# A two-layer MLA/NSA transformer kernel on one core: a PSUM place for each of four attention units, and transposes three units behind the scores

## The reference

```
for l in range(2):
    proj = rms_norm(x, attn_norm[l]) @ w_in[l]
    q_lat, kv_lat, k_rope, nsa_q, nsa_kv, gate_logits = split(proj)
    o_mla = mla_attention(...)      # 8 heads, causal softmax(q k) v, q and k built from q_lat, kv_lat, k_rope
    o_nsa = nsa_attention(...)      # 8 heads: compressed keys (31 blocks), selected blocks, window; gated sum
    x = x + concat([o_mla, o_nsa]) @ w_out[l]
    x = x + conv_ffn(rms_norm(x, ffn_norm[l]), ...)
return rms_norm(x, final_norm)
```

## Time and profile before

| | |
|---|---|
| time, median of 3 runs | 1435.41 us (1433.96 to 1436.16) |
| time of the profiled execution | 1435.41 us |
| its span in the trace | 1433.7 us |
| PE busy | 1333.7 us, 93% |
| DVE busy, ACT busy, POOL busy | 755.4, 650.3, 69.7 us |
| mean granted TensorE clock | 0.977 |

### The profile page before, as it was taken

How to read it: one execution, slowest core, us unless ns; L and a number is a source line. 1 busy time by engine, 2 the same in 40 slices (tenths; PEclk the granted TensorE clock), 3 DMA queues, 4 the chain that set the end, 5 groups by cost and what they waited for, 6 DMA issues and landing times.

```text
span 1433.7 us, 20017 instructions
## 1 busy us (share of the span) xinstructions
PE 1333.7 (93%) x6756; PEld 1079.0 (75%) x6756; DVE 755.4 (53%) x1200; ACT 650.3 (45%) x1173; POOL 69.7 (5%) x153
## 2 busy tenths in 40 slices
PE   5997888999999999999999988798999999999996
PEld 5995665567888888888889865566788888887884
DVE  6445566745455555533363646766364555564333
ACT  4345455744444544422352545666354454453222
POOL 1013001000000000000000401100000000000000
PEclk9998988999999999999999999989999999999998
DMA  6320100021433333323133101000323333323211
GB/s 202 114 81 2 59 1 1 16 89 54 120 89 114 90 88 108 112 89 101 52 100 95 51 18 43 1 16 1 118 76 113 90 88 105 100 88 117 88 59 59
DMA packets 121492, 107.69 MB, mean 75 GB/s; under 512 B 3874, under 2 KB 110980, under 8 KB 121424
## 3 DMA queue, kind: packets, MB, share of 16 engines
q1 hardware_dynamic: 119200, 102.71, 23.6%
q0 software_dynamic: 1360, 3.45, 0.9%
q10 hardware_dynamic: 864, 0.66, 0.1%
HBM read 104.71 MB, written 2.10 MB: 74 GB/s over the span
## 4 chain that ended last, share of the span: by engine, by line
PE 82%; DVE 7%; issue 5%; ACT 4%; DMA 1%; SPq 0%; DVEq 0%; ACTq 0%
PE ps L1306 23%; PE ps L1308 23%; PE ps L1307 23%; PE ps L1466 3%; PE ps L1507 3%; ACT probs L785 2%; PE ps L1490 1%; PE ps L1450 1%; PE ps L1542 1%; DVE probs L1115 1%; DMA raw<-in_w_in_dram 1%; PE ps L1451 1%; DVE x L986 1%; ACT probs_t L795 1%; DVE nmax L1097 1%
## 5 line engine op out<-in xcount | busy, mean ns | idle before, releaser
L1306 PE MATMUL ps<-ht_hi,w_hi 128*128 128x512 f32 (+2 forms) x776 | 299.9, 386 | 20.4 <-DVE k_operand L1139 5.3
L1308 PE MATMUL ps<-ht_hi,w_lo 128*128 128x512 f32 (+2 forms) x776 | 298.4, 385 | 0.0
L1307 PE MATMUL ps<-ht_lo,w_hi 128*128 128x512 f32 (+2 forms) x776 | 298.3, 384 | 0.0
L533 DVE TENSOR_TENSOR w_lo<-raw,w_hi 128x1024 fp32r<-128x1024 f32 (+4 forms) x196 | 218.1, 1141 | 105.0 <-ACT w_hi L526 97.2
L526 ACT ACTIVATE w_hi<-raw 128x1024 fp32r<-128x1024 f32 (+4 forms) x196 | 186.5, 982 | 109.2 <-PE ps L1308 103.8
L1251 DVE SCALAR_TENSOR_TENSOR conv<-ps,cols,conv 128x510 f32<-128x510 f32 (+1 forms) x176 | 127.7, 746 | 180.0 <-ACT conv L890 173.9
L1306 PEld LDWEIGHTS ps<-ht_hi,w_hi 128*128 128x128 f32 x776 | 146.7, 189 | 49.2 <-issue 17.5
L1308 PEld LDWEIGHTS ps<-ht_hi,w_lo 128*128 128x128 f32 x776 | 147.2, 190 | 28.1
L1307 PEld LDWEIGHTS ps<-ht_lo,w_hi 128*128 128x128 f32 x776 | 147.0, 189 | 27.5
L1306 PE MATMUL ps<-w_hi,ht_hi 128*128 128x430 f32 (+1 forms) x392 | 147.8, 377 | 5.9 <-DVE ht_lo L973 5.3
L1307 PE MATMUL ps<-w_lo,ht_hi 128*128 128x430 f32 (+1 forms) x392 | 145.4, 371 | 0.0
(11 more groups left out here) (182 smaller groups left out, 1705.1 us busy)
## 6 DMA issues: line engine op xcount, KB each, us to landing
raw<-in_ffn_w_up_dram SPq DMA_DIRECT2D x88, 512.0 KB, 4.3
raw<-in_ffn_w_down_dram SPq DMA_DIRECT2D x44, 512.0 KB, 3.6
raw<-in_w_in_dram SPq DMA_DIRECT2D x32, 430.0 KB, 3.4
raw<-in_w_out_dram SPq DMA_DIRECT2D x16, 512.0 KB, 4.7
raw<-in_nsa_cmp_w_dram SPq DMA_DIRECT2D x8, 512.0 KB, 4.2
x<-in_x_dram SPq DMA_DIRECT2D x4, 512.0 KB, 6.3
out_dram<-probs SPq DMA_DIRECT2D x4, 512.0 KB, 2.6
raw<-in_mla_w_uq_dram SPq DMA_DIRECT2D x4, 384.0 KB, 3.2
```

Source lines behind the costliest of these rows:

```text
L533: last = nc.vector.tensor_tensor(d(w_lo)[:, :, d0:d1], r(raw)[:, :, r0:r1], d(w_hi)[:, :, d0:d1].bitcast(F32), ALU.subtract)
L1306: mm(o, lhs[0], rhs[0], start=start, stop=False)
L1307: mm(o, lhs[0], rhs[1], start=False, stop=False)
L1308: return mm(o, lhs[1], rhs[0], start=False, stop=stop)
```

## The change

There are three edits that belong together, and several that follow from them.

1. Every unit gets a PSUM place by its query block: block 3 banks 0 and 1, block 2 banks 2 and 3, block 1 bank 4, block 0 bank 5. The transposes are written over the unit's own scores. So `scores(u)` now waits for `evac_pt(u - 4)`, and `turn(u)` waits for its probabilities alone.
2. `turn` moves from two to three steps behind the scores, `values` from four to five.
3. In each step the order is turned round. PE issues `queries` or `keys`, `turn(s - 3)`, `values(s - 5)`, the side job, and `scores(s)` last. ACT issues `evac_pt(s - 3)`, then the side splits, and `exps(s)` last. DVE takes the bank 7 work of the same step first, then `row_max(s)`, `q_lo`, `scale_probs(s - 1)`.

The rest: units with both heads in one bank write each head's causal mask by a product of its own (NSA's did it with one for both); `BACK_STEP`, `CS_MAX_STEP`, `CS_SCALE_STEP` and `PC_STEP` come two steps later; the four value products of MLA and their evacuations are taken in the order 3, 1, 0, 2.

```diff
-LAG = 4
+LAG = 5
+T_LAG = 3
-CS_STEP, BACK_STEP, CS_MAX_STEP, CS_SCALE_STEP, PC_STEP = [15, 18], [19, 20], 21, 23, [25, 26]
+CS_STEP, BACK_STEP, CS_MAX_STEP, CS_SCALE_STEP, PC_STEP = [15, 18], [21, 22], 23, 25, [27, 28]
+V_ORDER = (3, 1, 0, 2)
...
-            n = (unit(u)[0] + 1) * P
-            if u >= U_MLA and 2 * n <= S:
-                return ps[:, 2 * (u % 2), 0:2 * n].rearrange("p (a n) -> p a n", a=2)
-            return ps[:, 2 * (u % 2):2 * (u % 2) + 2, 0:n]
+            i = unit(u)[0]
+            n = (i + 1) * P
+            if i < 2:
+                return ps[:, 5 - i, 0:2 * n].rearrange("p (a n) -> p a n", a=2)
+            return ps[:, 6 - 2 * i:8 - 2 * i, 0:n]
...
-                    if u >= 2:
-                        pe.wait_ge(exp_done, at(exp_done, l, u - 1))
+                    if u >= T:
+                        pe.wait_ge(pt_done, at(pt_done, l, u - T + 1))
...
-                    if u >= 1:
-                        pe.wait_ge(pt_done, at(pt_done, l, u))
+                    sc = score_banks(u)
                     for s in range(2):
                         for b in range(i + 1):
-                            last = nc.tensor.transpose(ps[:, 4 + s, b * P:(b + 1) * P],
+                            last = nc.tensor.transpose(sc[:, s, b * P:(b + 1) * P],
```

More of the change, by code:

```diff
@@ L821, in _ @@
                 for s in range(U + LAG):
[L822 to L833, removed]
+                    if 0 <= s - T_LAG < U:
+                        evac_pt(s - T_LAG)
                     if LAG <= s < U_MLA + LAG and (s - LAG) % T == T - 1:
@@ L838, in _ @@
                         evac_out(H // 2 + pair, 6 + pair % 2)
-                    if not early and 0 <= s - 2 < U:
-                        evac_pt(s - 2)
+                    if s < QK_STEPS and s % T == 1:
+                        k_hi(s // T + 1, 7)
+                    if s < QK_STEPS and s % 2 == 0:
+                        q_hi(s // 2 + 2)
                     if s in ITEM_STEP:
@@ L865, in _ @@
                         activate(pct[:, g, :], ps[:, 7, :], ACT.Copy).then_inc(pct_ready, 1)
+                    if s < U:
+                        exps(s)
+                    if s == 2:
+                        act.wait_ge(gate_in, at(gate_in, l, 1))
+                        activate(gates[:, :, :], gate_e[:, :, :], ACT.Exp, scale=-1.0).then_inc(gate_exp, 1)
+                    if s == CS_MAX_STEP + 1:
+                        act.wait_ge(cs_sub, at(cs_sub, l, 1))
+                        activate(scp, scp, ACT.Exp).then_inc(cs_exp, 1)
                     if s == U_MLA + 4 * T:
@@ L1168, in _ @@
                 for s in range(U + LAG):
-                    if s < U:
-                        row_max(s)
-                    if s - 1 in ITEM_STEP:
-                        item_lo(ITEM_STEP.index(s - 1))
-                    if s == HIDT_STEP + 1:
+                    if s < QK_STEPS and s % 2 == 0:
+                        q_rows(s // 2 + 2, 7)
+                    if s < QK_STEPS and s % T == 1:
+                        k_lo(s // T + 1, 7)
+                    if s in ITEM_STEP:
+                        item_lo(ITEM_STEP.index(s))
+                    if s == HIDT_STEP:
                         dve.wait_ge(hid_tp, at(hid_tp, l, 1))
@@ L1602, in _ @@
                             queries(2 * pair + (s % T) // 2, 7)
-                    if s >= LAG and s not in VALUES_FIRST and s % 2 == 1:
+                    if 0 <= s - T_LAG < U:
+                        turn(s - T_LAG)
+                    if s >= LAG and (s - LAG) % 2 == 1:
                         values(s - LAG)
-                    if 0 <= s - 2 < U:
-                        turn(s - 2)
-                    if T <= s <= QK_STEPS:
+                    if T - 1 <= s <= QK_STEPS:
                         if s < QK_STEPS and s % T == 1:
```

101 lines of the change are left out of this document (43 added, 58 removed).

## The result

The changed kernel is slower. It took 1446.78 us (median of 4 runs, 1445.29 to 1447.34), the kernel before 1435.36 us beside it (4 runs, 1433.96 to 1436.16): ratio 1.0093, 95% interval 1.0077 to 1.0110, so 11.4 us more. I had forecast 1432.0: a small gain, and it is a loss. The range, 1413 to 1447 us, takes in the time at its very edge, and only because I had stretched it for the slower rival.

The account below looks back on a forecast made before the run. PE was taken as the bound (busy 1333.7 of 1433.7 us), so only its idle time, half-clock time and work count. Second part -4.4, first +2.7: -1.7 us a layer, -3.4 for both, from 1435.4 to 1432.0 us; range 1413 to 1447.

Parts of the forecast that it names:

- the slower rival: Whole kernel: bank 7 ring with ACT and DVE takes more than the quiet part gives back; 1447 us, chance 0.3.
- Second part: -4.4 us: Quiet NSA units and stage end, per layer: 3.7 us less idle, 1.2 from drains, 0.5 added by extra causal products.
- only one transpose still comes some 0.3 us early: Quiet part: `turn` of the 512-column unit waits for `scale_probs`; 0.3 us in 4.75 rounds, second part's idle 2.2 us.
- the drains that were to give 1.2 us: Second part: each wait uncovers a pipeline drain of 0.17 us; about seven fewer waits give 1.2 us.
- The extra masks' 0.5: Second part: about ten extra causal products at some 0.05 us each add 0.5 us.
- signs of being wrong: Among them, quiet part: DVE's `scale_probs` over 0.5 us late for every unit would make DVE's order the bound.
- the low clock I put at 11.5 instead of 12.5: First part: loss from PE's half clock falls from 12.5 to 11.5 us, as waits are fewer but longer.
- My bound of 6 us either way: First part: low-clock loss may lie between half and one and a half of 12.5 us.
- The first part's waits: Steps 0 to 28: PE's waits sum to 29.8 us, less 0.3 for the earlier start, against 24.8 before.
- the ring: Steps 12 to 18: `item_lo`, maxima, exponentials, copy, `item_hi` in turn, about 5.6 us; waits 7.6 us, before 6.4.
- Gain everywhere: Whole kernel: long waits too come from scarce places; first part idle 18 us, 1400 to 1420 us, chance 0.2.
- The rule of the Trainium skill: Quiet part: by the rule it gains clock as well as bubbles; the prediction's sum took bubbles alone, clock already 1.00.

Follow-up runs that it names:

- the run that prices them: The kernel before, with a causal product for each head in the small NSA units instead of one for both: 1434.24 us, ratio 1.0003.
- softmax run: The changed kernel, with return, maxima and scaling of the compressed scores one step earlier: 1435.24 us, ratio 1.0025 to the kernel before.
- order and distances alone: The changed kernel with the old PSUM banks (two score buffers, common transpose banks): 1459.29 us, ratio 1.0193 to the kernel before.
- the places alone: The kernel before with the new PSUM places and own causal masks, old step order and distances: 1425.12 us, ratio 0.9943.
- each mend: Four edits to the changed kernel: `k_hi` first, late items behind maxima, scaling ahead of 384-column maxima, softmax a step earlier; all four together 1424.20 us, ratio 0.9945.
- selective scaling: The changed kernel; from step 29 DVE scales the 256-column unit ahead of the 384-column unit's row maxima: 1437.03 us, ratio 1.0024 to the kernel before.
- key first: The changed kernel, with `k_hi` on ACT ahead of the exponentials of the step before: 1441.00 us, ratio 1.0060 to the kernel before.
- items behind the maxima: The changed kernel; from step 12 on DVE takes `item_lo` behind `row_max`: 1434.68 us, ratio 1.0016 to the kernel before.

## Why the prediction was wrong

- **The step that failed first** is "Second part: -4.4 us". I had laid the queues of four units beside each other and found "only one transpose still comes some 0.3 us early". I looked at the 512-column unit, where `scale_probs` stands behind its own exponentials. I overlooked that DVE's queue puts `row_max` of the 384-column unit ahead of `scale_probs` of the 256-column one, though that row maximum comes 3 us later than the exponentials are done. Idle fell from 5.9 to 4.3 and 4.7 us, not to 2.2. The waits did become seven fewer (8 instead of 15 in layer 0), as I had counted, but each is longer, and the drains that were to give 1.2 us did not show: busy time rose by 1.0 and 0.9 us. The extra masks' 0.5 is too small for the run that prices them (0.4 us for both layers, -1.1 to +2.0). In sum -0.6 and -0.4 instead of -4.4: 3.8 to 4.0 us a layer too good. That DVE's order made the waits is shown by moving the one call: 2.4 us idle. It brings the part to 57.6 us from the same scores, against 60.9 before, so 3.3 of the 4.4 us. The last 1.1 is mostly PE's busy time: 55.1 us, as before, where 0.7 less was forecast. What keeps it there stays open. My own list of signs of being wrong had this case, but only as one "for every unit"; one unit in four was enough.
- **The second** is the term "the low clock I put at 11.5 instead of 12.5". A mean clock of 0.88 over 143.1 us is 34 us at half clock where layer 0 had 30, and 0.87 over 141.9 in layer 1 is 37 where it had 24. By the prediction's own price (12.5 us of loss for 30) that is +1.6 and +5.2 us instead of -1.0. "Fewer but longer waits" was the wrong reason: there are fewer (17 instead of 24 in layer 0) and longer ones, and the low clock lasts longer. PE's busy time in this part rose by 0.6 and 3.9 us, where drains and clock were to take 2.0 off. The softmax run shows one such place, 13.6 us at 0.62 behind 4.4 us of idle time. My bound of 6 us either way did hold it.
- **The first part's waits** were right in sum in layer 0 (29.3 against 29.5; layer 1 had 28.0) and mostly one by one: 2.9 at step 2 (2.90), 4.2 at steps 5 and 9 (4.20, 4.12), 2.9 and 2.25 in the ring (2.70, 2.37), 2.5 ahead of `PC_STEP` (2.52), no `hid`. Off were the first item (3.0 for 2.0, since POOL's last rotation ended at 122.4 and the copy came behind it) and step 4 (1.35 for 2.0); the waits of 0.75 and 0.6 us that I had put into steps 6 to 11 of layer 0 did not come.
- **The account.** Forecast to measured span is 15.0 us: 7.8 from the second parts, 5.7 from the first (1.9 and 3.8), and 1.5 outside the stage, which the prediction had at nothing.
- **The slower rival** named 1447 us, and that is where the time came out, but not by its way: the ring of steps 12 to 18 added 1.3 us (7.7 against 6.4), not 3. The first part did lose more than the 4.4 us from which this rival decides (4.6 and 6.5), and the gain of the quiet part that I had set against it was missing. That the time fell on the rival's number is chance.
- **"Gain everywhere"** is refuted by the order and distances alone: with the old places the changed order is 27 us slower than before (1.9%). Its core, that the long waits come from scarce places, is wrong too: the places alone leave the waits for `hid` and for the items as they were, and gain in the quiet part and in PE's busy time (in all 8.0 us less busy, 0.6 less idle).
- **The rule of the Trainium skill** ("TensorE: Matmul & The Clock Gate", the second failure mode), by which small bubbles make the clock oscillate, got no support: the four quiet rounds are at 0.99 to 1.00 with waits of 0.3 to 0.6 us, and at 0.97 only where the waits reach 1.3 to 2.3 us (order and distances alone).

What stays open: how many microseconds of each mend are clock, and what the reversed queues cost apart from the longer distances. The sums of idle and busy time move against each other from run to run, and 4 of the 9.7 us of the selective scaling and most of what "key first" gained in layer 0 were won in code that they don't touch.

## What to carry to other kernels

Spare buffers give what they give only if the queues behind them let the producer run ahead: for each call on a helper engine ask when its input is ready, and whether a call whose input comes later stands ahead of it. Two engines that feed each other must each have the call that the other waits for first in the queue; swapped the wrong way round, they alternate instead of overlapping, here for 12 to 23 us. When a reversal is needed for one stage, time it apart from the buffers: here the buffers alone won 0.6%, and the reversal with its longer distances took 1.5% back. And before a gain is put down to an edit, look at which stretch became shorter.

## What the hardware showed that I had not expected

- The same waits cost more or less by where the low clock falls. The same 89 products of unchanged code took 23.5 us where 4.4 us of idle time fell into 10 us at full clock and the low clock came behind (0.62), and 20.1 us where the low clock came with the waits (0.65 in the first half, 1.00 in the second). With the wait for POOL gone they took 18.2 and 17.4. With the items behind the maxima 1.9 us less idle time went with 13.7 us less busy time.
- DVE's scaling of a 256-column unit takes 0.62 us in the quiet part, and took 2.22 us in one place where GpSimd cast keys at the same time, from 181.75 us for 2.12 us (items behind maxima, 181.81 us). That the cast is the cause is not shown.
- The first scores of the stage start at 109.96 and 109.97 us in two executions of the changed kernel, at 108.97 to 109.81 in variants whose code up to there is the same. I have no cause for it.
